# Expert products of a decoder trunk: three float32r products of halves become one plain float32 product

## Chip, cores and metric

One core of one Trainium2 chip runs the whole program. The metric is device time in microseconds (us) of that core for one launch, both layers of the trunk included; lower is better.

## What is computed

The program runs a trunk of two layers over 256 tokens of width 1024. Each layer has a mixer (four head groups) and a channel part, PEER: 8 heads choose 16 of 16384 single-neuron experts per token, and their outputs are summed. With `t` the 256 x 1024 normed activations:

```python
q = (t @ w_q).reshape(T, PEER_HEADS, 2, PEER_DKEY // 2)          # 1024 -> 2048
s1 = einsum('thd,kd->thk', q[:, :, 0], sk1)                      # 128 keys each side
s2 = einsum('thd,kd->thk', q[:, :, 1], sk2)
# top 16 of each side, top 16 of the 256 sums -> expert, gate (softmax)
a = einsum('td,thkd->thk', t, u_tab[expert])
w = gate * gelu(a)
y = einsum('thk,thkd->td', w, v_tab[expert])
```

The kernel doesn't gather. It multiplies all 16384 rows of `u_tab` with `t`, applies gelu, multiplies by a gate grid that is zero for experts not chosen, and multiplies by all of `v_tab`. All is float32. Before each layer, six modulation vectors (`silu(c) @ ada_w`, 1024 x 6144) are needed.

## The kernel before

All large weights lie in one stream of blocks of 128 x 1024 float32 (512 KB). SP fetches them in order into a ring of 4 slots (`ring`), each fetch behind a semaphore that says that the slot's block was used. Per layer there are 33 blocks for the mixer, 16 for `w_q` (query blocks), 128 for `u_tab` (expert rows) and 128 for `v_tab` (value rows). Another 48 blocks for layer 0's modulation come first; layer 1's 48 are fetched into the two slots of `ada_ring` during layer 0's value rows.

Mixer blocks are multiplied as they are, as plain float32 (lines 1278, 1290, 1478): 8 matmuls of a 128 x 128 weight with a 128 x 256 moving tile (`hT`, the normed activations, or `ynT`).

Query, expert and value blocks are multiplied in halves. A number is split in a float32r part (`hi`) and the rest (`lo`, float32r too), and each product is three float32r matmuls, hi x hi, hi x lo, lo x hi (`exact`, lines 1487 to 1491). ScalarE writes `split_hi` from the ring (`high`, line 688; line 763 for value rows). GpSimd subtracts to write `split_lo` for query and expert blocks and the first four value blocks (line 471), VectorE for the other value blocks (line 1169). The moving side is split, too: `h_hi` and `h_lo` by VectorE once a layer (1078, 1079), `w_hi` by ScalarE (757, 764) and `w_lo` by VectorE (1163, 1170) per value block. Both halves have 4 slots. A ring slot is free when its `lo` has been written.

The order of a layer on TensorE: mixer; output projection (1478); sum of squares `ss2` (1233); query blocks, each pair followed by the key scores of the pair before it (1507), which ScalarE copies out (531); expert rows in 16 turns of 8 blocks, each pair of blocks followed by a gelu on ScalarE (715) into `grid`, while VectorE chooses the top 16s from `scores`; gate grids (1556), made from one-hot tiles of VectorE (1135, 1137), ScalarE (740, 743) and GpSimd (482), which VectorE multiplies into `grid` (1142); value rows, which accumulate in four banks of PSUM that a product with `zeros` opens (1569); then VectorE adds the result to `xT` (1179). Each engine has its own instruction queue, in the order written.

In layer 0's value rows (loops of 20 blocks) GpSimd multiplies the eight `ada_ring` blocks of each of six turns by `silu(c)` and adds them to `ada_acc` (493 to 498). TensorE then sums the columns (`ada_sums`, 1241). In layer 0's own modulation at the start VectorE does it with one fused operation per block (841, 843).

`tables` (relative bias and rotary tables) and `KM` (masks) lie where the halves lie. So `tables` is spilled to DRAM in layer 0 and read back for layer 1, and `KM` is loaded twice.

Of the kernel before, what the change touches and what calls it, by code (L numbers as in the profile page):

```python
# [18 lines left out]
F32 = mybir.dt.float32  # L19
F32R = mybir.dt.float32r  # L20
# [6 lines left out]
P = 128  # L27
# [23 lines left out]
RING = 4  # L51
SPLIT = 4
# [19 lines left out]
EARLY = PQ + KEYS + SPLIT  # L72
LATE = KEYS - SPLIT
# [84 lines left out]
def build(nc, stream, s5w, consts, mixc, small, vec, pos, x_in, out):  # L158
    with ExitStack() as ctx:
# [17 lines left out]
        split_hi = at_byte("split_hi", 16 * KB, [SPLIT, BLOCK], F32R)  # L177
        split_lo = at_byte("split_lo", 32 * KB, [SPLIT, BLOCK], F32R)
        tables = at_byte("tables", 16 * KB, [HEADS * (P + T) + 3 * T])
        KM = at_byte("KM", 26 * KB, [N_MIXC])  # L180
        s5raw = at_byte("s5raw", 32 * KB, [1024])

        hT = at_byte("hT", 48 * KB, [KT, T])
        h_hi = at_byte("h_hi", 48 * KB, [KT, T], F32R)
        w_hi = at_byte("w_hi", 48 * KB, [SPLIT, T], F32R)
        w_lo = at_byte("w_lo", 52 * KB, [SPLIT, T], F32R)

        stage = at_byte("stage", 56 * KB, [2048])
        h_lo = at_byte("h_lo", 56 * KB, [KT, T], F32R)
# [130 lines left out]
        ge = at_byte("ge", 32 * KB, [FIRST, P + T], F32R)  # L320
# [58 lines left out]
        spilled, mixc_in, tables_in = (sem(n) for n in ("spilled", "mixc_in", "tables_in"))  # L379
        ada_used, ada_scaled, ada_columns = (sem(n) for n in ("ada_used", "ada_scaled", "ada_columns"))  # L380
        ada_filled = [sem(f"ada_filled{i}") for i in range(2)]
        hi_ready, lo_ready, h_split = sem("hi_ready"), sem("lo_ready"), sem("h_split")
        vhi_ready, v_ready, v_used = sem("vhi_ready"), sem("v_ready"), sem("v_used")
        hot_eq, hot_step, column_ready, turned_picks = (sem(n) for n in ("hot_eq", "hot_step", "column_ready", "turned_picks"))
        spill = nc.dram_tensor("spill", (P, HEADS * (P + T) + 3 * T), F32).ap()
# [7 lines left out]
        def early_at(l):  # L393

            return mix_at(l) + MIX


        @block.sync
        def _(sp):
# [26 lines left out]
            for l in range(DEPTH):  # L426
                segment(mix_at(l) + RING, MIX, block_used, l * MIX)
                segment(early_at(l) + RING, EARLY, lo_ready, l * EARLY)
                late = early_at(l) + EARLY
                if l + 1 == DEPTH:  # L430
                    segment(late + RING, LATE - RING, v_ready, l * KEYS + SPLIT)
                    break

                sp.wait_ge(w_ready, T // 4 * (l + 1))
                ada_turns = (0, 1, 4, 6, 8, 10, 12, 14)
                with sp.Fori(0, ADA // KT, 1) as i:
                    for j in range(20):
                        sp.wait_ge(v_ready, i * 20 + (l * KEYS + SPLIT + j + 1))
                        fetch(i * 20 + (late + RING + j), (late + RING + j) % RING)
                        if j in ada_turns:  # L440
                            k = ada_turns.index(j)
                            sp.wait_ge(ada_used, i * 8 + (ADA + k - 1))
                            sp.dma_start(ada_ring[:, k % 2, :], stream[bass.ds(i * 8 + (N_MAIN + l * ADA + k), 1)]
                                         .rearrange("o p c -> (o p) c")).then_inc(ada_filled[k % 2], 16)
                segment(late + RING + 120, LATE - 120, v_ready, l * KEYS + SPLIT + 120)
# [6 lines left out]
        def _(pool):  # L452
            gp = nc.gpsimd
            for l in range(DEPTH):
# [12 lines left out]
                e0 = early_at(l)  # L467

                def low(i, j):
                    pool.wait_ge(hi_ready, i * SPLIT + (l * EARLY + j + 1))  # L470
                    gp.tensor_tensor(split_lo[:, j, :], ring[:, (e0 + j) % RING, :], split_hi[:, j, :].bitcast(F32), ALU.subtract)\  # L471
                        .then_inc(lo_ready, 1)

                with pool.Fori(0, EARLY // SPLIT, 1) as i:
                    for j in range(SPLIT):
                        low(i, j)

# [6 lines left out]
                if l + 1 < DEPTH:  # L484

                    with pool.Fori(0, ADA // KT, 1) as i:
                        for k in range(KT):
                            pool.wait_ge(ada_filled[k % 2], i * (16 * KT // 2) + 16 * (k // 2 + 1))
                            silu = siluc[:, k:k + 1].broadcast_to([P, BLOCK])
                            if k == 0:  # L490

                                pool.wait_ge(ada_columns, i + ADA // KT)
                                gp.tensor_tensor(ada_acc[:, :], ada_ring[:, 0, :], silu, ALU.mult).then_inc(ada_used, 1)
                            else:
                                b = ada_ring[:, k % 2, :]
                                gp.tensor_tensor(b, b, silu, ALU.mult).then_inc(ada_scaled, 1)
                                pool.wait_ge(ada_scaled, i * (KT - 1) + k)
                                gp.tensor_tensor(ada_acc[:, :], ada_acc[:, :], b, ALU.add).then_inc(ada_used, 1)  # L498
                            pool.wait_ge(ada_used, i * KT + (ADA + k + 1))
# [16 lines left out]
        def _(act):  # L516
# [55 lines left out]
            for l in range(DEPTH):  # L572
                act.wait_ge(small_in, 16)
                if l:

                    act.wait_ge(v_used, l * KEYS)
                act.dma_start(s5raw[:, :], s5w[l]).then_inc(s5w_in, 16)
                if l:
                    act.dma_start(KM[:, :], mixc).then_inc(mixc_in, 16)
                    act.dma_start(tables[:, :], spill).then_inc(tables_in, 16)  # L580
# [92 lines left out]
                if l == 0:  # L673
                    act.wait_ge(t5_ready, HEADS)
                    act.wait_ge(rope_ready, 1)
                    act.dma_start(spill, tables[:, :]).then_inc(spilled, 16)

# [3 lines left out]
                e0 = early_at(l)  # L681
                if l == 0:
                    act.wait_ge(spilled, 16)

                def high(n, i=0, turn=0):

                    act.wait_ge(slot_filled[(e0 + n) % RING], i * (16 * turn // RING) + 16 * ((e0 + n) // RING + 1))
                    nc.scalar.activation(split_hi[:, n % SPLIT, :], ring[:, (e0 + n) % RING, :], ACT.Copy).then_inc(hi_ready, 1)  # L688


                for n in range(SPLIT - 1):
                    high(n)
                root(l, "ss2", D, rstd)
                for k in range(KT):
                    act.wait_ge(xr_ready, 2 * KT * l + KT + k + 1)
                    nc.scalar.activation(sq[:, k, :], sq[:, k, :], ACT.Identity, bias=mod2[:, l, 3 * KT + k:3 * KT + k + 1],
                                         scale=sc2[:, k:k + 1]).then_inc(h_ready, 1)
                high(SPLIT - 1)
                for h in range(PH + 1):
                    for w in range(2):  # L700
                        if h < PH:
                            copy(l, f"pq{h}_{w}", qT[:, 2 * (h % 2) + w, :])
                            high(2 * h + w + SPLIT)
# [6 lines left out]
                def gelus(i):  # L710
                    for j in range(4):
                        act.wait_ge(a_ready, i * 4 + (first + j + 1))
                        for w in range(2):
                            high(PQ + 2 * j + w + SPLIT, i, 8)
# [39 lines left out]
                act.wait_ge(w_ready, T // 4 * (l + 1))  # L754
                late = e0 + EARLY
                for j in range(SPLIT):
                    nc.scalar.activation(w_hi[:, j, :], grid[:, j * T:j * T + T], ACT.Copy).then_inc(vhi_ready, 1)
                with act.Fori(0, LATE // SPLIT, 1) as i:
                    for j in range(SPLIT):
                        s = (late + j) % RING  # L760
# [967 lines left out]
```

## Time and profile before

| | us |
|---|---|
| median of 3 runs | 2529.12 (2522.28 to 2531.38) |
| span of the profiled execution | 2525.9 |
| TensorE busy (matmul records) | 2230.9, 88% |
| VectorE busy | 1553.5, 62% |
| ScalarE busy | 1185.2, 47% |
| GpSimd busy | 1123.5, 44% |
| bytes moved | 378.58 MB, mean 150 GB/s |

The profiled execution's span lies 3.2 us below the median of the runs. Stages in its time: modulation and tables to 130, mixer and output projection to 337, query blocks 347 to 414, expert rows to 784, gate grids to 910, value rows to 1344; then the same without the first: mixer to 1569, query blocks 1579 to 1646, expert rows to 2016, gate grids to 2142, value rows to 2511, final norm to 2526. Of the profile's page, the chain of waits gives 19% to GpSimd's `split_lo` and 7% to each of the three product lines. In the rows below the engines are PE (TensorE's matmuls), PEld (its weight loads), DVE (VectorE), ACT (ScalarE), POOL (GpSimd) and SP (SyncE, which issues the DMAs).

### The profile page before, as it was taken

Reading aid. Unit: us, or ns where it says so; the run is one execution under the profiler, and the core shown is the slowest. Engines: PE = TensorE matmul, PEld = TensorE weight load, DVE = VectorE, ACT = ScalarE, POOL = GpSimd, SP = SyncE. Lnnn points to the kernel's source line nnn. Section 1 sums busy time; section 2 is a strip of 40 time slices with the busy share of each in tenths; the row PEclk is TensorE's granted clock in tenths of the full one; section 3 lists DMA queues with packets and bytes.
Section 4 is the critical chain, followed back from the end, with each engine's and each line's share of the span. In section 5 each row is a group of like instructions: output and inputs, shape, how many; then the busy total and the mean of one; then the engine's idle time right before and its main releaser. Section 6 shows DMA issues by size and latency. Waiting matters only on the chain.

```text
span 2525.9 us, 46629 instructions
## 1 busy us (share of the span) xinstructions
PE 2230.9 (88%) x16556; PEld 2138.3 (85%) x16556; DVE 1553.5 (62%) x2319; ACT 1185.2 (47%) x2092; POOL 1123.5 (44%) x472
## 2 busy tenths in 40 slices
PE   5797789999997589999998967999999956999998
PEld 4686679999996588989997856899999955999998
DVE  7577348993004977888885952699800088555554
ACT  8522434555545743333433232455554476444443
POOL 0002036988886545555550301588988854000000
PEclk9798789999998999999998987999999999999999
DMA  7632144555553036556553312345555500555553
GB/s 264 216 115 78 45 141 134 183 179 187 183 181 102 0 116 218 206 209 224 208 215 120 125 34 92 125 151 190 181 180 181 182 17 0 175 182 182 183 183 108
DMA packets 103456, 378.58 MB, mean 150 GB/s; under 512 B 11489, under 2 KB 11873, under 8 KB 102881
## 3 DMA queue, kind: packets, MB, share of 16 engines
q1 hardware_dynamic: 102672, 373.74, 43.3%
q10 hardware_dynamic: 720, 4.00, 0.4%
q8 instruction: 40, 0.66, 0.1%
q14 instruction: 24, 0.19, 0.0%
HBM read 375.46 MB, written 2.23 MB: 150 GB/s over the span
## 4 chain that ended last, share of the span: by engine, by line
PE 34%; issue 24%; POOL 23%; DVE 12%; DMA 3%; ACT 2%; POOLq 1%; DVEq 1%; SPq 0%; ACTq 0%
POOL split_lo L471 19%; PE bank L1489 7%; PE bank L1490 7%; PE bank L1491 7%; PE bank L1556 3%; PE bank L1278 3%; POOL hots L482 2%; DVE w_lo L1170 2%; DMA ring<-stream 1%; DVE hots L1137 1%; PE bank L1241 1%; DVE split_lo L1169 1%; POOL ada_acc L498 1%; DMA ada_ring<-stream 1%; DVE hots L1135 1%
## 5 line engine op out<-in xcount | busy, mean ns | idle before, releaser
L471 POOL TENSOR_TENSOR split_lo<-ring,split_hi 128x1024 fp32r<-128x1024 f32 x296 | 729.3, 2489 | 246.6 <-ACT split_hi L688 246.3
L1489 PE MATMUL bank<-h_hi,split_hi 128*128 128x256 f32 x2304 | 657.0, 285 | 29.7 <-DVE h_lo L1079 21.3
L1490 PE MATMUL bank<-h_lo,split_hi 128*128 128x256 f32 x2304 | 654.4, 284 | 0.0
L1491 PE MATMUL bank<-h_hi,split_lo 128*128 128x256 f32 x2304 | 654.4, 284 | 0.0
L1489 PE MATMUL bank<-w_hi,split_hi 128*128 128x256 f32 x2048 | 589.4, 288 | 14.2 <-DVE w_lo L1170 14.2
L1490 PE MATMUL bank<-w_lo,split_hi 128*128 128x256 f32 x2048 | 586.8, 287 | 0.0
L1491 PE MATMUL bank<-w_hi,split_lo 128*128 128x256 f32 x2048 | 586.5, 286 | 0.0
L1169 DVE TENSOR_TENSOR split_lo<-ring,split_hi 128x1024 fp32r<-128x1024 f32 x248 | 375.3, 1513 | 251.6 <-ACT w_hi L764 251.6
L1489 PEld LDWEIGHTS bank<-h_hi,split_hi 128*128 128x128 f32 x2304 | 444.5, 193 | 34.7 <-issue 18.6
L763 ACT ACTIVATE split_hi<-ring 128x1024 fp32r<-128x1024 f32 x248 | 262.5, 1059 | 448.9 <-PE bank L1491 416.0
L1491 PEld LDWEIGHTS bank<-h_hi,split_lo 128*128 128x128 f32 x2304 | 444.8, 193 | 0.0
L1490 PEld LDWEIGHTS bank<-h_lo,split_hi 128*128 128x128 f32 x2304 | 444.8, 193 | 0.0
L688 ACT ACTIVATE split_hi<-ring 128x1024 fp32r<-128x1024 f32 x296 | 298.4, 1050 | 274.0 <-PE bank L1491 273.7
L1489 PEld LDWEIGHTS bank<-w_hi,split_hi 128*128 128x128 f32 x2048 | 400.8, 196 | 17.1 <-DVE w_lo L1170 17.1
L1490 PEld LDWEIGHTS bank<-w_lo,split_hi 128*128 128x128 f32 x2048 | 400.8, 196 | 0.1
L1491 PEld LDWEIGHTS bank<-w_hi,split_lo 128*128 128x128 f32 x2048 | 400.6, 196 | 0.0
L1135 DVE TENSOR_TENSOR hots<-K,pick 128x256 f32<-128x256 f32 x64 | 54.1, 846 | 307.4 <-ACT pick L732 224.5
L1556 PE MATMUL bank<-hots 128*128 128x128 f32 x1024 | 137.8, 291 | 105.8 <-POOL hots L482 105.8
L1556 PEld LDWEIGHTS bank<-hots 128*128 128x128 f32 x1024 | 126.5, 202 | 117.1 <-DVE grid L1142 88.3
L1170 DVE TENSOR_TENSOR w_lo<-grid,w_hi 128x256 fp32r<-128x256 f32 x248 | 188.6, 760 | 0.0
L482 POOL TENSOR_TENSOR hots<-hots,pick 128x1024 f32<-128x1024 f32 x64 | 123.3, 1928 | 103.9 <-DVE hots L1137 103.9
L740 ACT ACTIVATE hots<-K,pick 128x128 f32<-128x128 f32 x384 | 119.1, 388 | 56.0 <-PE bank L1556 56.0
(267 smaller groups left out, 2776.9 us busy)
## 6 DMA issues: line engine op xcount, KB each, us to landing
ring<-stream SPq DMA_DIRECT2D x658, 512.0 KB, 3.3
ada_ring<-stream SPq DMA_DIRECT2D x48, 512.0 KB, 4.8
spill<-tables ACTq DMA_DIRECT2D x1, 1152.0 KB, 5.4
tables<-spill ACTq DMA_DIRECT2D x1, 1152.0 KB, 7.2
xT<-x_in SPq DMA_DIRECT2D x1, 1024.0 KB, 10.2
s5raw<-s5w ACTq DMA_DIRECT2D x2, 512.0 KB, 5.7
y_out<-hT SPq DMA_DIRECT2D x1, 1024.0 KB, 3.9
KM<-mixc SPq DMA_DIRECT2D x1, 576.0 KB, 8.3
```

The source lines that it names most:

```text
L471: gp.tensor_tensor(split_lo[:, j, :], ring[:, (e0 + j) % RING, :], split_hi[:, j, :].bitcast(F32), ALU.subtract)\
L482: gp.tensor_tensor(hotA[j], hotA[j], pick[:, 2, bass.ds(i * 16 + 8 * j, 8)].unsqueeze(2).broadcast_to([P, 8, P]), ALU.mult).then_inc(hot_r ...
L688: nc.scalar.activation(split_hi[:, n % SPLIT, :], ring[:, (e0 + n) % RING, :], ACT.Copy).then_inc(hi_ready, 1)
L740: last = nc.scalar.activation(hotB[j][:, t, :], iota, ACT.Abs, scale=-1.0, bias=pick[:, 1, bass.ds(n * 8 + t, 1)])
L763: nc.scalar.activation(split_hi[:, j, :], ring[:, s, :], ACT.Copy)
L1135: v.tensor_tensor(hotB[j][:, 0:2, :], iota.unsqueeze(1).broadcast_to([P, 2, P]), pick[:, 1, bass.ds(n * 8, 2)].unsqueeze(2).broadcast_to([ ...
L1169: v.tensor_tensor(split_lo[:, j, :], ring[:, (late + j) % RING, :], split_hi[:, j, :].bitcast(F32), ALU.subtract)
L1170: v.tensor_tensor(w_lo[:, j, :], grid[:, bass.ds(i * (SPLIT * T) + (SPLIT + j) * T, T)], w_hi[:, j, :].bitcast(F32), ALU.subtract).then_in ...
L1489: mm(dst, hi, x_hi, start=start, stop=False, skip_group_check=not group)
L1490: mm(dst, hi, x_lo, start=False, stop=False, skip_group_check=not group)
L1491: return mm(dst, lo, x_hi, start=False, stop=stop, skip_group_check=not group)
L1556: last = mm(bank[:, j, t * P:t * P + P], hotB[j // 2][:, s, :], hotA[j // 2][:, s, :], start=True, stop=True)
```

## The change

The three products of halves become one plain float32 matmul of the ring's block with `hT` (query and expert rows) or with `grid` (value rows). The second sub-layer's norm is written to `hT` instead of `sq`. All splits go, on ScalarE, GpSimd and VectorE. The space of `split_hi` goes to the ring, which has 8 slots; the ring's fetches now all wait for `block_used`, which TensorE raises. `tables` and `KM` get a place of their own for the whole run: no spill, no reload. `s5raw` moves to the bytes of `hots0`, `ge` to those of `stage` and its neighbours. Layer 1's modulation moves from GpSimd to VectorE, with one fused operation per block; turns of value rows have 16 blocks instead of 20, and each `ada_ring` load is issued behind every second fetch.

```diff
-RING = 4
-SPLIT = 4
+RING = 8
+TURN = 16
@@ SP @@
-                    for j in range(20):
-                        sp.wait_ge(v_ready, i * 20 + (l * KEYS + SPLIT + j + 1))
-                        fetch(i * 20 + (late + RING + j), (late + RING + j) % RING)
-                        if j in ada_turns:
-                            k = ada_turns.index(j)
+                    for j in range(TURN):
+                        sp.wait_ge(block_used, i * TURN + (freed + MIX + PQ + KEYS + j + 1))
+                        fetch(i * TURN + (v0 + RING + j), (v0 + RING + j) % RING)
+                        if j % 2 == 0:
+                            k = j // 2
                             sp.wait_ge(ada_used, i * 8 + (ADA + k - 1))
                             sp.dma_start(ada_ring[:, k % 2, :], stream[bass.ds(i * 8 + (N_MAIN + l * ADA + k), 1)]
@@ ScalarE @@
-                    act.wait_ge(v_used, l * KEYS)
+                    act.wait_ge(w_ready, T // 4 * l)
                 act.dma_start(s5raw[:, :], s5w[l]).then_inc(s5w_in, 16)
-                if l:
-                    act.dma_start(KM[:, :], mixc).then_inc(mixc_in, 16)
-                    act.dma_start(tables[:, :], spill).then_inc(tables_in, 16)
...
-                    nc.scalar.activation(sq[:, k, :], sq[:, k, :], ACT.Identity, bias=mod2[:, l, 3 * KT + k:3 * KT + k + 1],
+                    nc.scalar.activation(hT[:, k, :], sq[:, k, :], ACT.Identity, bias=mod2[:, l, 3 * KT + k:3 * KT + k + 1],
@@ VectorE, value rows @@
-                            v.tensor_tensor(split_lo[:, j, :], ring[:, (late + j) % RING, :], split_hi[:, j, :].bitcast(F32), ALU.subtract)
...
+                if l + 1 < DEPTH:
+                    with dve.Fori(0, ADA // KT, 1) as i:
+                        for k in range(KT):
+                            dve.wait_ge(ada_filled[k % 2], i * (16 * KT // 2) + 16 * (k // 2 + 1))
...
+                                ins = v.scalar_tensor_tensor(ada_acc[:, :], ada_ring[:, k % 2, :], siluc[:, k:k + 1], ada_acc[:, :],
+                                                             ALU.mult, ALU.add)
@@ TensorE @@
-                        last = exact(dst, hi[:, k, :], lo[:, k, :], h_hi[:, k, :], h_lo[:, k, :], k == 0, k == KT - 1)
+                        last = mm(dst, b[:, k, :], hT[:, k, :], start=(k == 0), stop=(k == KT - 1))
...
-                            last = exact(bank[:, 4 + m // 2, (m % 2) * T:(m % 2) * T + T], split_hi[:, s, c], split_lo[:, s, c],
-                                         w_hi[:, s, :], w_lo[:, s, :], False, False, group=False)
-                        last.then_inc(v_used, 1)
+                            last = mm(bank[:, 4 + m // 2, (m % 2) * T:(m % 2) * T + T], ring[:, slot, m * P:m * P + P],
+                                      grid[:, bass.ds(i * (n * T) + j * T, T)], start=False, stop=False, skip_group_check=True)
+                        last.then_inc(block_used, 1)
```

## Rows read from the trace of the kernel before

**Rows 1.** The page: GB/s moved, in 40 equal slices of the span.
```profile
GB/s 264 216 115 78 45 141 134 183 179 187 183 181 102 0 116 218 206 209 224 208 215 120 125 34 92 125 151 190 181 180 181 182 17 0 175 182 182 183 183 108
```

**Rows 2.** Busy time by stretch: length, busy us (records) per engine, clock, DMA share, GB/s.
```profile
415.00:788.00 373.00, 368.98 (x3075) 368.71 (x3073) 176.93 (x305) 195.59 (x227) 315.05 (x128) 1.00 0.54 179
910.00:1344.00 434.00, 403.91 (x3167) 399.86 (x3167) 344.19 (x249) 169.30 (x248) 224.97 (x90) 0.95 0.59 208
2142.00:2512.00 370.00, 368.99 (x3074) 368.76 (x3072) 194.70 (x251) 169.65 (x250) 0.00 (x0) 1.00 0.50 170
```

**Rows 3.** TensorE in order of time, expert rows: start, length, what, [idle before].
```profile
414.34 0.39 PE L1489 MATMUL bank<-h_hi,split_hi 128*128 128x256 f32 x1 [0.47 <-ACT grid L531]
...
700.02 0.28 PE L1489 MATMUL bank<-h_hi,split_hi 128*128 128x256 f32 x1
700.14 0.28 PE L1490 MATMUL bank<-h_lo,split_hi 128*128 128x256 f32 x1
```

**Rows 4.** Lines 1278 and 1478 alone: records, ns min/median/max, first and last start.
```profile
L1278 PE MATMUL bank<-hT,ring x512: 379/379/796, 130.0 to 1448.8; 128*128 128x256 f32 x171
...
L1478 PE MATMUL bank<-hT,ring x256: 379/379/796, 304.0 to 1566.2; 128*128 128x256 f32 x128
```

**Rows 5.** TensorE in order of time, mixer of layer 0.
```profile
153.46 13.98 PE L1278 MATMUL bank<-hT,ring 128*128 128x256 f32 x64
167.28 3.62 PE L1303 MATMUL bank<-grid,ring 128*128 128x256 f32 x16
170.73 7.31 PE L1290 MATMUL bank<-ring,hT 128*128 128x128 f32 x64
```

**Rows 6.** TensorE's groups, 910 to 1344 us: records, busy, mean ns, idle before.
```profile
L1489 PE MATMUL bank<-w_hi,split_hi 128*128 128x256 f32 x1024 | 299.4, 292 | 14.2 <-DVE w_lo L1170 14.2
...
L1241 PE MATMUL bank<-K,ada_acc 128*128 128x1 f32 x96 | 15.8, 294 | 15.9 <-POOL ada_acc L498 15.9
```

**Rows 7.** Busy time by stretch behind two of the six column sums, columns as before.
```profile
978.00:980.00 2.00, 2.00 (x12) 2.00 (x11) 0.00 (x0) 0.00 (x0) 0.00 (x0) 0.50 0.85 283
...
1047.00:1050.00 3.00, 3.00 (x16) 3.00 (x16) 1.14 (x2) 0.00 (x0) 0.00 (x0) 0.50 0.91 285
```

**Rows 8.** Order of time at three handoffs: mixer, query blocks, gate grids of layer 0.
```profile
130.01 1.22 PE L1278 MATMUL bank<-hT,ring 128*128 128x256 f32 x2 [6.96 <-ACT hT L588]
...
346.94 0.55 PE L1489 MATMUL bank<-h_hi,split_hi 128*128 128x256 f32 x1 [8.94 <-DVE h_lo L1079]
...
784.01 2.00 ACT L688 ACTIVATE split_hi<-ring 128x1024 fp32r<-128x1024 f32 x2 [3.27 <-PE bank L1491]
...
785.92 0.58 ACT L715 ACTIVATE grid<-bank 128x512 f32 x1
786.40 1.85 ACT L740 ACTIVATE hots<-K,pick 128x128 f32<-128x128 f32 x6
...
788.28 0.84 ACT L743 ACTIVATE hots<-hots 128x768 f32<-128x768 f32 x1
...
789.95 4.73 POOL L482 TENSOR_TENSOR hots<-hots,pick 128x1024 f32<-128x1024 f32 x2
792.92 6.01 PE L1556 MATMUL bank<-hots 128*128 128x128 f32 x32 [8.95 <-POOL hots L482]
```

**Rows 9.** Line 1137 alone, ns min/median/max.
```profile
L1137 DVE TENSOR_TENSOR hots<-K,pick x64: 1209/1212/3422, 741.7 to 2132.4; 128x1024 f32<-128x1024 f32 x64
```

**Rows 10.** Line 843 alone, and its idle time before (us, times).
```profile
L843 DVE SCALAR_TENSOR_TENSOR grid<-ring,tiny,grid x42: 1278/1285/1286, 22.5 to 99.0; 128x1024 f32 x42
...
  DMA ring<-stream: 6.4, 12
```

**Rows 11.** DMA issues: count, KB each, median us to landing.
```profile
ring<-stream SPq DMA_DIRECT2D x658, 512.0 KB, 3.3
ada_ring<-stream SPq DMA_DIRECT2D x48, 512.0 KB, 4.8
```

**Rows 12.** Line 1241 alone: the register operations of TensorE's sequencer.
```profile
L1241 PEldq FUSED_REGOPS  x48: 42/46/51, 974.3 to 1317.0; - x48
```

## What the change should do

> **What bounds the kernel now.** I read four views, in this order. The first is the table by stretch [rows 2], which tells what each stage costs and which engine fills it. In the expert products of layer 0 (415 to 788 us) TensorE is busy 369 of 373 us at granted clock 1.00, and in the value products of layer 1 (2142 to 2512) 369 of 370 us. GpSimd is busy 315 of 373 us in the first and not at all in the second, and the time per block is the same. So GpSimd, which the chain of waits names most often, is close behind but is not the limit: TensorE is. A block there is 24 matmuls. The value products of layer 0 take 434 us for the same 128 blocks, because they also hold the next layer's modulation sums.
>
> Second is the order of instructions on TensorE. In a dense stretch a float32r matmul starts every 0.12 us [rows 3], so a block costs 24 x 0.12 = 2.88 us. Check against the stage: 128 blocks x 2.88 = 368.6 us, and layer 1's value products keep TensorE busy for 369.0 us [rows 2].
>
> Third is the price of what replaces them, a plain float32 128x128 by 128x256 matmul. The mixer's projections are just that, from the same ring and with the same moving tile hT. Here the count must be read before the duration. Line 1278 is called for 16 projections per layer, 8 matmuls each, 2 layers: 256 matmuls. The trace has 512 records [rows 4]. Line 1478 has 8 x 8 x 2 = 128 matmuls and 256 records [rows 4]. So one plain float32 matmul is two records, each with its own weight load. 64 records start from 153.46 and the next line's from 167.28 [rows 5]: 13.82 / 64 = 0.216 us for a record, 0.432 us for a matmul, 8 x 0.432 = 3.455 us for a block. The trap is to read 0.216 us as a whole matmul.
>
> Beside the rows: the Trainium skill, "FP8 and Floating Point Precision", section "TensorE Precision Notes", says that true FP32 takes 4 passes through the array. By that rule alone a block would be 32 passes against the 24 of the three-product form, a third more. The rows give 3.455 / 2.88 = 1.20, since the float32r matmul with its 0.120 us is dearer than a quarter of 0.432. Sum by the rule's ratio: 544 blocks x 0.96 us = +522 us instead of +313. The measured pace decides, and I go by it.
>
> **The change part by part.**
>
> (a) Products. Each of the 544 blocks (per layer 16 query blocks, 128 expert rows, 128 value rows) goes from 2.88 to 3.455 us of TensorE, +0.575. Where TensorE is the limit this is all on the path. Expert rows: layer 0 runs from 414.34 to 783.97 (the first grid matmul at 792.92 less its 8.95 idle) [rows 3, 8], 369.6 us; new 128 x 3.455 = 442.3. +73 a layer, +146 for both. Value rows of layer 1: 369 to 442.3, +73.5.
>
> (b) Halves. On ScalarE, GpSimd and VectorE 544 `split_hi`, 296 + 248 `split_lo` and 248 pairs of `w_hi`/`w_lo` go away. The busiest of the three, GpSimd, took 315.05 / 128 = 2.46 us per block [rows 2] beside TensorE's 2.88, so removing them returns only the 14.2 us that TensorE waited for `w_lo` in layer 0's value rows [rows 6]. What is late next is TensorE itself.
>
> (c) Value rows of layer 0. Now 434 us [rows 2]: 368.6 of products, 15.8 of column sums (line 1241), 15.9 waiting for `ada_acc`, 14.2 for `w_lo` [rows 6]; the remaining 19.5 us is what the clock costs after the pauses. It stands near 0.50 for 3 to 7 us behind them (two such stretches: [rows 7]), where a product takes twice as long. After the change the sums move from GpSimd to VectorE, one fused operation per block. The same form takes 1.28 us [rows 10], so 8 are 10 us in a turn of 55 us: hidden. The wait doesn't go, however. The eighth `ada_ring` load is issued only when block 14 of the turn is used, and only block 15 (3.46 us) stands before the sums. SP's two issues and its wake are about 0.5 us, an estimate, the landing 4.8 us [rows 11], the operation 1.28, some 0.2 for semaphores, an estimate too: 6.8 us, so a stall of 3.3 us, x 6 = 20 us. Bounds: 2 us each if it lands in the ring's 3.3 [rows 11], so 12, and 4.5 each, so 27. I keep the clock's 19.5 us, since pause and column sums stay as long. New: 442.3 + 15.8 + 20 + 19.5 = 497.6, +63.6 (55 to 75). SP queues the ring's next fetch ahead of the late load and nothing urgent behind it, with eight slots ahead.
>
> (d) Query stage. Now 67.4 us (346.94 to 414.34). New: 16 x 3.455 = 55.3; the keys' 64 records a layer at 0.114 us, the pace of 64 plain 128-column records in the mixer [rows 5], 7.3; half clock at the start about 2, waits for ScalarE's copies about 4, both estimates: 68.6. +1 a layer, between -4 and +4.
>
> (e) Handoff to the query stage. Now TensorE idles 8.94 us behind `h_lo`, while the same chain without halves at the start of the mixer costs 6.96 us [rows 8]. -2 a layer, -4; the later waits for `h_lo` (about 1.8 us a layer) are inside the range.
>
> (f) Start of the gate grids. The last products end at 783.97, yet ScalarE's last gelu starts at 785.92, since two `split_hi` stand before it; the first grid waits for GpSimd's `hots`, behind two `split_lo`, at 789.95 [rows 8]. Without these: gelu 0.58, six one-hots 1.85 and the Relu 0.84, about 3.4 us to the first grid matmul. VectorE's one-hot line 1137 took up to 3.42 us, just there, against 1.21 normally [rows 9], and its GpSimd neighbour is gone, too. -5.5 a layer, -11 (-4 to -12). By the Trainium skill, "SBUF — State Buffer", section on the two separate sides, a GpSimd operation and certain VectorE ones hold a shared port exclusively; the 3.42 us fits, and elsewhere in the change it touches nothing on the path. The rest of the grid stage (one turn of 7 us per two quads) has the same operations.
>
> (g) Ring of 8, at the start: VectorE's fused operations wait 6.4 us for the ring [rows 10], and the plain ones before them 2 to 3 more. Eight slots may take half of it, while `pos` now shares its landing with more loads: -4 (-9 to +3). A block of 0.524 MB per 3.455 us is 152 GB/s, less than the 170 to 208 of the stages now [rows 2], so no stage becomes bound by transfers; with 48 more in (c) it is 185.
>
> (h) The spill, its reload, KM's reload and their waits: no wait for them is among TensorE's or VectorE's in these stretches, so 0 (-2 to 0).
>
> (i) The moving operand of the value rows is now addressed by a register. No row shows that on TensorE; the nearest is line 1241 on `ada_acc`, one register operation of 46 ns per matmul [rows 12]. Its upper bound is 2048 x 0.046 = 94 us. Line 1241's 96 records still take only 15.8 us [rows 6], 0.33 us a matmul with clock losses, and 46 ns fits into 432: 0.
>
> Sum: 146 + 73.5 + 63.6 + 2 - 4 - 11 - 4 = +266. Profiled span 2525.9 + 266 = 2792 us; the median of runs lies 3.2 us above the profiled span, so **2795 us**.
>
> **Rivals.**
> A, not slower: one float32 matmul is one record of 0.216 us, so a block costs 1.73 us. Transfers would bound it before that: 0.524 MB at 264 GB/s, the fastest slice of the profile [rows 1], is 1.99 us. 544 x (2.88 - 1.99) = 484 us less, some 2045 us. It decides at a block cost of 2.88 us, that is 0.36 us a matmul. For it: GpSimd, the chain's top entry, is freed. Against: 512 records for 256 calls, and the same for line 1478. 2%.
> B: register addressing of the moving operand isn't hidden, up to +94, so up to 2889. Against: line 1241's pace. 4%.
> C: layer 0's value rows go without stall and clock loss, since the turn is regular and GpSimd no longer feeds them: -39, 2756. Against: the load that is issued one block ahead. 6%.
> D: a price that follows the count of passes (4 to 3) as in the four products of halves against three: +0.96 us a block instead of 0.575, 544 x 0.385 = +209, some 3000 us. Against: the measured pace of line 1278 under traffic. 2%.
>
> **How the numbers follow.** Forecast as summed 86%. The bounds together: (c) -8 to +11, (d) +-8, (f) -1 to +7, (g) -5 to +7, expert rows +-6. Added as independent about +-18, and widened for what I can't see; with C the range reaches 2755 to 2835. A measurement of this kernel can tell about 0.5% from no change; 2795 is 10.5% above. Slower 0.97, within 0.5% 0.01, faster 0.02.
>
> **What would show it.** In the profile of the changed kernel: 16 records per block at 0.216 us on the two product lines (4096 records for the value rows and 4608 for query and expert rows); expert rows about 442 us with TensorE busy throughout at clock 1.00; 6 stalls of about 3.3 us at the column sums with the clock at 0.5 behind each; GpSimd with no work in expert and value rows; first grid matmul 3.4 us after the last product. 8 records per block would prove A; gaps of 40 to 50 ns between value matmuls B.

## The result

The changed kernel takes 2779.6 us (median of 4 runs, 2774.2 to 2784.7) against 2525.7 us for the kernel before (4 runs). The ratio is 1.101, with a 95% interval of 1.098 to 1.103. The forecast of 2795 us was 0.6% too high, and the time lies in the forecast range of 2755 to 2835 us. The profiled execution has a span of 2779.5 us, 253.6 more than before. The page of the changed kernel, parts 1 to 4, first lines (line 1412 is the query and expert product, line 1500 the value product, 1475 the gate grids, 1160 the column sums):

```profile
span 2779.5 us, 33968 instructions
...
PE 2527.7 (91%) x12204; PEld 2210.0 (80%) x12204; DVE 882.6 (32%) x1831; ACT 533.8 (19%) x1268; POOL 167.3 (6%) x86
...
PE 81%; DVE 9%; issue 3%; ACT 2%; POOL 2%; DMA 1%; DVEq 0%; SPq 0%; POOLq 0%; ACTq 0%
PE bank L1412 36%; PE bank L1500 32%; PE bank L1475 2%; PE bank L1197 2%; PE bank L1397 2%; POOL hots L465 2%; DVE hots L1057 1%; PE bank L1160 1%; DVE grid L774 1%; DMA ada_ring<-stream 1%; PE bank L1371 1%; PE bank L1152 1%; DVE hots L1055 1%; PE bank L1422 1%; PE bank L1222 0%
```

Every engine except TensorE has lost much of its work: ScalarE 1185 to 534 us, GpSimd 1124 to 167, VectorE 1554 to 883. TensorE has 297 us more, and now it holds 81% of the chain. So a quarter fewer matmul records (16556 to 12204) cost more time, since a plain record takes 0.216 us and a float32r record 0.120.

The table by stretch of the changed kernel (length, busy us and records of PE, PEld, DVE, ACT, POOL, then granted clock, DMA share, GB/s), for layer 0's expert rows, layer 0's value rows and layer 1's value rows, which answer to [rows 2]:

```profile
404.00:847.00 443.00, 442.90 (x2054) 389.60 (x2054) 93.22 (x307) 55.57 (x80) 1.90 (x1) 1.00 0.46 152
966.00:1463.00 497.00, 479.47 (x2146) 419.46 (x2144) 58.90 (x50) 0.00 (x0) 0.00 (x0) 0.95 0.54 185
2322.00:2764.00 442.00, 442.00 (x2050) 389.09 (x2049) 0.00 (x0) 0.00 (x0) 0.00 (x0) 1.00 0.44 143
```

TensorE in order of time, layer 1's value rows, which answers to [rows 3, 5]:

```profile
2322.31 442.19 PE L1500 MATMUL bank<-grid,ring 128*128 x2048
```

The two product lines alone (records, ns min/median/max, first and last start), which answer to [rows 4]:

```profile
L1500 PE MATMUL bank<-grid,ring x4096: 379/379/774, 966.2 to 2764.1; 128*128 x196
...
L1412 PE MATMUL bank<-hT,ring x4608: 379/379/795, 335.7 to 2202.3; 128*128 128x256 f32 x192
```

There are 16 records per block, 4096 for 256 value blocks and 4608 for 288 query and expert blocks, and 442.19 / 2048 = 0.216 us per record. Neither line waits inside a stage: the 4608 records of line 1412 have 14.9 us of idle time before them in total, almost all of it at the two starts.

Where the 253.6 us come from, stage by stage, worked out from the first starts and the idle times in both traces:

| stage | before | after | difference | forecast |
|---|---|---|---|---|
| start to output projection, layer 0 | 304.0 | 294.6 | -9.4 | -4 |
| output projection to query blocks, layer 0 | 43.0 | 41.1 | -1.9 | -2 |
| query blocks, both layers | 134.8 | 135.8 | +1.0 | +2 |
| expert rows, layer 0 / 1 | 369.6 / 369.6 | 443.0 / 443.0 | +73.3 / +73.3 | +73 / +73 |
| gate grids, layer 0 / 1 | 125.9 / 126.0 | 119.3 / 119.6 | -6.6 / -6.4 | -5.5 / -5.5 |
| value rows, layer 0 | 434.6 | 496.5 | +61.9 | +63.6 |
| mixer to query blocks, layer 1 | 234.6 | 229.5 | -5.1 | -2 |
| value rows, layer 1 | 369.0 | 442.2 | +73.2 | +73.5 |

### The profile page after: what moved, and what is told of

Read it like the earlier page. It is cut to its first block, busy times and chain, and to the rows that moved or that the text cites. A ratio compares the mean times of both kernels' runs of the same rounds, so it can differ in the third digit from the quotient of the medians.

```text
span 2779.5 us, 33968 instructions
## 1 busy us (share of the span) xinstructions
PE 2527.7 (91%) x12204; PEld 2210.0 (80%) x12204; DVE 882.6 (32%) x1831; ACT 533.8 (19%) x1268; POOL 167.3 (6%) x86
## 3 DMA queue, kind: packets, MB, share of 16 engines
q10 hardware_dynamic: 288, 1.05, 0.1%
HBM read 373.70 MB, written 1.05 MB: 135 GB/s over the span
## 4 chain that ended last, share of the span: by engine, by line
PE 81%; DVE 9%; issue 3%; ACT 2%; POOL 2%; DMA 1%; DVEq 0%; SPq 0%; POOLq 0%; ACTq 0%
PE bank L1412 36%; PE bank L1500 32%; PE bank L1475 2%; PE bank L1197 2%; PE bank L1397 2%; POOL hots L465 2%; DVE hots L1057 1%; PE bank L1160 1%; DVE grid L774 1%; DMA ada_ring<-stream 1%; PE bank L1371 1%; PE bank L1152 1%; DVE hots L1055 1%; PE bank L1422 1%; PE bank L1222 0%
## 5 line engine op out<-in xcount | busy, mean ns | idle before, releaser
L1412 PE MATMUL bank<-hT,ring 128*128 128x256 f32 x4608 | 1002.7, 380 | 14.9 <-ACT hT L643 13.9
L1412 PEld LDWEIGHTS bank<-hT,ring 128*128 128x128 f32 x4608 | 877.5, 191 | 135.5 <-ACT hT L643 14.7
L1500 PE MATMUL bank<-grid,ring 128*128 x4096 | 902.0, 384 | 0.0
L1500 PEld LDWEIGHTS bank<-grid,ring 128*128 128x128 f32 x4096 | 789.5, 193 | 110.2
L658 ACT ACTIVATE grid<-bank 128x512 f32 x128 | 76.4, 597 | 625.6 <-PE bank L1412 625.3
L1197 PE MATMUL bank<-hT,ring 128*128 128x256 f32 x512 | 119.5, 396 | 16.0 <-ACT hT L552 13.9
L1089 DVE SCALAR_TENSOR_TENSOR ada_acc<-ada_ring,tiny,ada_acc 128x1024 f32<-128x1024 f32 x42 | 54.0, 1285 | 236.6 <-DMA ada_ring<-stream 236.6
L1197 PEld LDWEIGHTS bank<-hT,ring 128*128 128x128 f32 x512 | 101.4, 199 | 33.9 <-ACT hT L552 14.7
L1062 DVE TENSOR_TENSOR grid<-grid,bank 128x512 f32 (+1 forms) x128 | 87.9, 688 | 25.4 <-PE bank L1475 24.6
L1171 PE MATMUL bank<-ge,diag 128*128 128x384 f32 x248 | 54.0, 366 | 36.9 <-ACT diag L522 25.4
L1171 PEld LDWEIGHTS bank<-ge,diag 128*128 128x128 f32 x248 | 45.8, 203 | 44.8 <-issue 25.8
L1057 DVE TENSOR_TENSOR hots<-K,pick 128x1024 f32<-128x1024 f32 x64 | 77.6, 1213 | 0.0
L1397 PE MATMUL bank<-hT,ring 128*128 128x256 f32 x256 | 60.1, 400 | 1.4 <-ACT hT L477 1.4
## 6 DMA issues: line engine op xcount, KB each, us to landing
KM<-mixc SPq DMA_DIRECT2D x1, 576.0 KB, 11.1
```

The lines of the kernel that those rows point to most:

```text
L658: nc.scalar.activation(grid[:, bass.ds(i * (8 * T) + j * 2 * T, 2 * T)], bank[:, j, :], ACT.Gelu_apprx_tanh).then_inc(gelu_done, 1)
L1057: v.tensor_tensor(hotA[j], iota.unsqueeze(1).broadcast_to([P, 8, P]), pick[:, 0, bass.ds(n * 8, 8)].unsqueeze(2).broadcast_to([P, 8, P]), ...
L1062: v.tensor_tensor(gw, gw, bank[:, b, :].rearrange("p (t a) -> p a t", t=4), ALU.mult).then_inc(w_ready, 1)
L1171: last = mm(bank[:, 2 + q, 0:P + T], diag[:, j, q, part, :], ge[:, slot, :], start=isinstance(b, int) and b + part == 0, stop=False, skip_ ...
L1197: last = mm(r, b[:, k, :], hT[:, k, :], start=(k == 0), stop=(k == KT - 1))
L1397: last = mm(r, b[:, k, :], ynT[:, k, :], start=(k == 0), stop=(k == KT - 1))
```

## Experiments

Each ran against the kernel before on the same chip. Theory: TensorE's price per block sets the stages with products; pauses at the column sums come from the late load and cost their own length and a stretch of half clock; the deeper ring helps at the start only. The rivals are those of the prediction and, for the kernel before, that GpSimd was the limit.

### One part alone: plain products in layer 1's value rows of the kernel before

```diff
...
+                            for m in range(KT):
+                                last = mm(bank[:, 4 + m // 2, (m % 2) * T:(m % 2) * T + T], ring[:, s, m * P:m * P + P],
+                                          grid[:, bass.ds(i * (SPLIT * T) + (SPLIT + j) * T, T)], start=False, stop=False,
+                                          skip_group_check=True)
+                            last.then_inc(v_used, 1)
```

(and the loops that make the halves of these blocks taken out; TensorE waits for the ring's slot itself, and SP's fetches wait for `v_used`)

> The kernel before with one part of the change: layer 1's value blocks 4 to 127 as plain float32 matmuls from the ring (4 slots), without their halves; all else as before. Theory (only TensorE's price per block counts): 124 x 0.575 = +71 us, the value rows from 369 to 440, 2526 + 71 = 2597 in all. Rival (the halves on ScalarE and VectorE had cost something in hidden waits or contention, so that the net is smaller): under +60.

Measured: 2596.6 us against 2525.4, ratio 1.027 (1.025 to 1.030), so +71 us. The new line alone, in that kernel:

```profile
L1600 PE MATMUL bank<-grid,ring x1984: 377/379/381, 2153.4 to 2581.4; 128*128 x199
L1600 PEldq FUSED_REGOPS  x124: 46/46/65, 2151.5 to 2574.3; - x124
```

1984 records for 124 blocks, from 2153.4 to the end of the last at about 2581.7: 3.454 us a block. The price shows by itself, with the ring of 4 and everything else of the kernel before. The halves of these blocks are gone from ScalarE and VectorE, and no gain from that comes off it: the rival (under +60 us) falls.

### The moving operand at a fixed address

```diff
-                                      grid[:, bass.ds(i * (n * T) + j * T, T)], start=False, stop=False, skip_group_check=True)
+                                      grid[:, j * T:j * T + T], start=False, stop=False, skip_group_check=True)
```

> The changed kernel with the moving operand of the value rows at an address that doesn't depend on the loop's register (it reads the same 16 columns of the grid in every turn, so the sum is another). Theory (the register operation is hidden under the 0.432 us of a matmul): 442 us for layer 1's value rows, 2780 in all. Rival B of the prediction (it costs up to 46 ns a matmul): 2048 x 0.046 = 94 us less, 2686.

Measured: 2773.5 us (two runs) against the changed kernel's 2779.6. Layer 1's value rows in order of time, in this kernel:

```profile
2315.43 442.19 PE L1500 MATMUL bank<-grid,ring 128*128 128x256 f32 x2048
```

The same 442.19 us as with the register. The 6 us between the two kernels are the width of the spread of the runs (2774 to 2785), and in the profiled executions they lie in layer 0's value rows (490.6 instead of 496.5 us), where the clock falls at other moments. Rival B falls. The records of the sequencer also show that its premise was wrong: 124 register operations for 124 blocks above, and 256 for 256 blocks in the changed kernel, one per block and not one per matmul.

### A ring of 4 slots in the changed kernel

```diff
-RING = 8
+RING = 4
...
-                    pe.wait_ge(slot_filled[slot], i * 16 + 16 * (n // RING + 1))
+                    pe.wait_ge(slot_filled[slot], i * (16 * 8 // RING) + 16 * (n // RING + 1))
...
-                    for j in range(RING):
+                    for j in range(8):
```

> The changed kernel with a ring of 4 slots again. Theory (the deeper ring helps only at the start, where VectorE waited 9.1 us for blocks): the query stage starts 8 to 10 us later, 2788 to 2790 in all, expert and value rows unchanged at 443, 496 and 442 us. Rival (the ring isn't what shortened the start; the order of the first loads is): within 2 us of 2780. Rival (with 4 slots the 3.46 us blocks also stall in layer 0's value rows, where two streams share the transfers): 10 to 30 us there.

Measured: 2782.2 us median (2779.3 to 2794.1, 5 runs), ratio to before 1.101 (1.099 to 1.104). In the profiled execution the query stage starts at 345.35 us instead of 335.72, and VectorE waits for the ring again. Waits of VectorE, 15 to 110 us, with 4 slots:

```profile
DVE grid L774 <- DMA ring<-stream: 7.9, 15, 1.0
...
DVE grid L772 <- DMA ring<-stream: 1.4, 2, 0.7
```

With 8 slots that view has no wait for the ring in this stretch. So the 9.4 us at the start are the ring's by the profiles. The medians don't show it: they differ by 2.6 us only, which their spreads don't tell apart, and the expected 2788 to 2790 us was missed. The profile with 4 slots is also that of its slowest run. Layer 0's value rows take 498 instead of 497 us, with 19.2 instead of 17.2 us at the column sums: the second rival falls, too.

### The modulation loads earlier, in the changed kernel

```diff
-                        if j % 2 == 0:
-                            k = j // 2
+                        if j in (0, 1, 2, 4, 6, 8, 10, 12):
+                            k = (0, 1, 2, 4, 6, 8, 10, 12).index(j)
```

> The changed kernel with the eight loads of layer 1's modulation blocks issued behind fetches 0, 1, 2, 4, 6, 8, 10, 12 of a turn instead of 0, 2, ..., 14. Value rows of layer 0 take 496.5 us in the changed kernel: 442.2 of products, 20.3 of column sums, 17.2 of waiting for ada_acc, 16.8 left over, which I put down to the clock. Theory (the late load is what TensorE waits for, and its pause is what lowers the clock): the wait goes to 0, the leftover goes too, and the sums take 12: 455 to 462, the run at about 2742. Rival 1 (the sums with one moving column lower the clock by themselves): only the wait goes, 479, the run at about 2762. Rival 2 (VectorE's own sums are late, not the load): nothing moves, 2780.

Measured: 2737.4 us (4 runs), ratio to before 1.084 (1.081 to 1.086), 42 us less than the changed kernel. First the changed kernel around a column sum, in order of time and by stretch (0.50 is 1.2 GHz, 1.00 is 2.4 GHz):

```profile
1016.12 1.28 DVE L1089 SCALAR_TENSOR_TENSOR ada_acc<-ada_ring,tiny,ada_acc 128x1024 f32<-128x1024 f32 x1 [5.53 <-DMA ada_ring<-stream]
1018.90 0.33 SPq L436 DMA_DIRECT2D ada_ring<-stream  x1
...
1023.07 1.28 DVE L1089 SCALAR_TENSOR_TENSOR ada_acc<-ada_ring,tiny,ada_acc 128x1024 f32<-128x1024 f32 x1 [5.67 <-DMA ada_ring<-stream]
1024.49 3.57 PE L1160 MATMUL bank<-K,ada_acc 128*128 128x1 f32 x16 [2.90 <-DVE ada_acc L1089]
```

```profile
1021.00:1024.00 3.00, 0.59 (x3) 0.19 (x1) 0.93 (x1) 0.00 (x0) 0.00 (x0) 0.99 0.84 292
1024.00:1028.00 4.00, 3.51 (x17) 3.51 (x17) 0.36 (x1) 0.00 (x0) 0.00 (x0) 0.50 0.11 43
1028.00:1031.00 3.00, 3.00 (x9) 2.44 (x9) 0.00 (x0) 0.00 (x0) 0.00 (x0) 0.53 0.00 0
```

The last load is issued at 1018.90, VectorE can start on it 4.2 us later, and TensorE's pause until it has finished is 2.90 us. Then the clock stands at its lower level for some 7 us: the sum takes 3.57 us, and 9 product records fall in 3 us, where the run with earlier loads has 16 in a stretch of the same length. Behind the first two of the six pauses the lower level lasts about 7 us, behind the other four about 10. The third sum starts at 1151.13, and the clock has fallen before that, while TensorE still does nothing (busy 0.00):

```profile
1150.00:1151.00 1.00, 0.00 (x0) 0.00 (x0) 0.99 (x1) 0.00 (x0) 0.00 (x0) 0.63 0.95 369
```

So it is in five of the six turns; in the second the clock falls during the sum. With the earlier loads, the same views (two of the six sums, and the stretches around the first):

```profile
1020.72 1.84 PE L1160 MATMUL bank<-K,ada_acc 128*128 128x1 f32 x16
1077.76 1.84 PE L1160 MATMUL bank<-K,ada_acc 128*128 128x1 f32 x16
```

```profile
1020.00:1023.00 3.00, 3.00 (x24) 2.85 (x23) 0.00 (x0) 0.00 (x0) 0.00 (x0) 1.00 0.43 122
1023.00:1026.00 3.00, 3.00 (x16) 2.64 (x15) 0.00 (x0) 0.00 (x0) 0.00 (x0) 1.00 0.24 97
```

No pause, full clock through the sum, and the six sums follow each other at 57.04 us: 55.34 for 16 blocks and 1.70 from the first matmul of a sum to the next product. Value rows take 453 us (1.00, busy throughout) instead of 496.5. So rival 1 falls: the one-column sums don't lower the clock by themselves. The pause of 2.8 to 3.0 us goes ahead of the fall each time, and it costs more than its own length: 17.2 us of waiting stood for 43.5, of which 9 lay in the sums (20.3 to 11.1) and 17 in the products behind them. Not every such pause lowers it at once: behind the value rows the changed kernel pauses 3.39 us before the sum of squares, and the clock stays at 1.00 through it.

### The same shift in the kernel before

```diff
-                ada_turns = (0, 1, 4, 6, 8, 10, 12, 14)
+                ada_turns = (0, 1, 3, 5, 7, 9, 11, 12)
```

> The kernel before with the eight loads of layer 1's modulation blocks behind fetches 0, 1, 3, 5, 7, 9, 11, 12 of the 20 of a turn instead of 0, 1, 4, 6, 8, 10, 12, 14. There TensorE waits 15.9 us for ada_acc in layer 0's value rows and some 19.5 us more go to the clock behind it. Theory (the late load is the cause here, too, and the clock follows the pause): the last load comes two blocks, 5.8 us, earlier against waits of 2.65 us each, so up to 35 us less, 2490. Rival (GpSimd's own 5.3 us per block is what is late, in a turn where it waits 16 us for its first load but not for its last): the wait stays or shrinks by a third, 2515 to 2525. Rival (the fetch queue blocks on the ada slot and the ring of 4 runs dry): slower than 2530.

Measured: 2503.5 us (2495.6 to 2510.9, 6 runs) against 2525.8, ratio 0.992 (0.990 to 0.995). The wait for `ada_acc` is gone, as the theory says, and value rows take 410.5 us instead of 434.6. But the expected 35 us came to 22 in the run and 24 in this stage. TensorE's waits in that stretch:

```profile
PE bank L1489 <- DVE w_lo L1170: 21.4, 19, 2.2
```

It was 14.2 us [rows 6], so 7 us of the gain went into a wait that was there before. And of the 20 us that were left over in this stage, 9 stay. The granted clock still falls three times, for 3.4 us each and each time around a wait for `w_lo` of 2.0 to 2.2 us. That is some 5 us of lost products, an estimate; the other 4 have no account. ScalarE's waits for the ring grew from 32.9 to 80.2 us; the ring of 4 with its fetches behind the crowded loads is a likely reason for the longer waits, but no run tests it. This version is 0.8% faster than the kernel before, with the same three products, and beats the changed one.

### Two products instead of three, in the kernel before

```diff
                     mm(dst, hi, x_hi, start=start, stop=False, skip_group_check=not group)
-                    mm(dst, hi, x_lo, start=False, stop=False, skip_group_check=not group)
                     return mm(dst, lo, x_hi, start=False, stop=stop, skip_group_check=not group)
```

> The kernel before without the second of the three products (high half of the block by low half of the moving side), in query, expert and value rows; all halves are still made. It leaves that part of the sum out. TensorE's block falls from 2.88 to 16 x 0.12 = 1.92 us. Theory (TensorE was the limit, and GpSimd with 2.46 us is next in expert rows, VectorE with 1.51 + 0.76 = 2.27 in value rows): expert rows 128 x 2.6 = 333 instead of 370, value rows of layer 1 about 300 instead of 369; 2526 - 74 - 69 - 10 to 30 = about 2360. Rival (GpSimd was already the limit, as the chain's 19% suggests): expert rows stay at 370. Rival (halves cost nothing at all): 246 us for each stage, 2526 - 0.96 x 544 = 2004.

Measured: 2245.4 us, ratio 0.890 (0.885 to 0.896). By stretch: layer 0's query and expert rows, and layer 1's value rows.

```profile
342.00:715.00 373.00, 327.90 (x2374) 300.82 (x2374) 275.38 (x479) 223.79 (x273) 350.00 (x143) 0.97 0.60 199
1995.00:2234.00 239.00, 239.00 (x1994) 238.99 (x1992) 190.72 (x245) 165.90 (x244) 0.00 (x0) 1.00 0.81 263
```

144 query and expert blocks take 371 us instead of 437, with GpSimd busy 94% of it. The 128 expert rows alone take 318.5 instead of 369.6 us: 2.49 us a block, GpSimd's own pace (2.46 before). So GpSimd was second, 0.4 us a block behind TensorE, and it is the limit once TensorE's share falls. It was not the limit before, or this stage would not have moved. In layer 1's value rows, where VectorE makes the low halves, TensorE is busy throughout and 1994 records fill 239 us, 0.120 us each: 1.92 us a block, so there TensorE is still the limit. My 2.27 us for VectorE was too high there: its 190.72 us for the 245 operations of this stretch are 1.56 us a block. That stage gives 123 us where the forecast of this run had 69, and query and expert rows give 131 where it had 74. Together they are 111 of the 115 us between 2360 and 2245.

Layer 0's value rows gave only 19 us (415.7 instead of 434.6). TensorE waits 74.5 us there for VectorE's `w_lo`. VectorE is slower in that stage, where GpSimd works beside it. In the kernel before, its subtraction alone, in layer 0's value rows and then in layer 1's (count, busy us, mean ns, idle before):

```profile
L1169 DVE TENSOR_TENSOR split_lo<-ring,split_hi 128x1024 fp32r<-128x1024 f32 x124 | 223.2, 1800 | 83.4 <-ACT w_hi L764 83.4
...
L1169 DVE TENSOR_TENSOR split_lo<-ring,split_hi 128x1024 fp32r<-128x1024 f32 x124 | 152.1, 1227 | 168.2 <-ACT w_hi L764 168.2
```

So in layer 0's value rows VectorE was the close second before, with 2.78 us a block (344.19 / 124 [rows 2]) against 2.88.

### One product of the high halves

```diff
-                    mm(dst, hi, x_hi, start=start, stop=False, skip_group_check=not group)
-                    mm(dst, hi, x_lo, start=False, stop=False, skip_group_check=not group)
-                    return mm(dst, lo, x_hi, start=False, stop=stop, skip_group_check=not group)
+                    return mm(dst, hi, x_hi, start=start, stop=stop, skip_group_check=not group)
```

(and the loops that make the low halves of blocks and of `w` taken out; the waits that named a low half, SP's fetches among them, name the high half)

> The kernel before with only the product of the two high halves, and no low halves of blocks made (GpSimd's and VectorE's subtractions are gone, w_lo too). It leaves the other two products out. TensorE 8 x 0.12 = 0.96 us per block, ScalarE 1.05 for the half and 0.3 to 0.37 for the gelu or w_hi. Theory (transfers bound it next): at the 264 to 315 GB/s of the fastest slices a block takes 1.66 to 1.99 us, so expert rows 213 to 255 us, value rows the same, about 1950 to 2050 in all. Rival (the handover between ScalarE and ring with 4 slots bounds it, since a transfer takes 3.3 us to land): 128 x 3.5 / 4 + waits, under 200 us. Rival (ScalarE's chain): 128 x 1.4 = 180 us.

Measured: 1860.3 us, ratio 0.737 (0.735 to 0.740). By stretch: layer 0's query and expert rows, its value rows, layer 1's value rows.

```profile
342.00:597.00 255.00, 183.81 (x1222) 162.53 (x1221) 133.70 (x475) 215.99 (x267) 1.90 (x1) 0.93 0.82 286
722.00:1030.00 308.00, 189.01 (x1114) 177.56 (x1113) 0.21 (x1) 162.90 (x248) 190.30 (x90) 0.73 0.80 289
1640.00:1845.00 205.00, 159.06 (x1032) 136.94 (x1031) 0.00 (x0) 163.99 (x248) 0.00 (x0) 0.96 0.87 307
```

The expected 1950 to 2050 us was missed. No compute engine is full: TensorE has 184 of 255 us, ScalarE 216. The DMA share is 0.80 to 0.87, and 286 to 307 GB/s arrive in all three, with 332 in the fastest slice of its page. A block takes 1.60 to 1.77 us (layer 0's value rows count 176, with the modulation's), below the 1.99 of rival A's bound, which took the 264 GB/s of one slice [rows 1] for a limit. So TensorE is no longer the limit, and transfers are the likely one, but that isn't shown. In layer 0's query and expert rows ScalarE waits only 21.2 us for the ring, so it is close to the limit itself. And a ring load lands in 4.9 us here instead of 3.3: with 4 slots and 1.05 us of ScalarE for each, the handover rival gives (4.9 + 1.05) / 4 = 1.5 us a block, an estimate near the measured pace. No run with a deeper ring tells the two apart. This version computes with the rounding of float32r in all three kinds of block; where that is enough, it is the fastest by far.

## Why the prediction held, point by point

**What bounds the kernel.** TensorE was the limit in the product stages. Adding 0.575 us a block to TensorE, with less work for all others, moved them by 0.573 (73.3 / 128), and taking 0.96 away moved the expert rows by 0.40, down to GpSimd's pace. The chain's 19% for `split_lo` was a close second's share.

**(a), the price of a block.** Two records per plain matmul is the step that carried the forecast: with 0.216 us read as a whole matmul, rival A came to 484 us less, not 254 more. The 3.455 us came out in three kernels (the changed one, the one with the fixed address, the one with plain products in layer 1's value rows alone). Rival A and rival D (passes counted without durations) both fall. "FP8 and Floating Point Precision" of the Trainium skill, section "TensorE Precision Notes", by its 4 passes, has the direction right; the ratio is 1.20 here and not 4 / 3, as each float32r matmul takes 0.120 us where half a plain record takes 0.108.

**(b), halves.** Right in the main: the engines' 650 to 960 us of busy time came back as little more than the 14 us of waits. Two readings were off. The busiest of the three isn't GpSimd everywhere: in layer 0's value rows it is VectorE, 2.78 us a block, since its subtraction takes 1.80 us there and 1.23 in layer 1, without GpSimd beside it. So (f)'s remark that this neighbour touches nothing on the path elsewhere doesn't hold: the 14.2 us of waits for `w_lo` are all in that stage, and layer 1's value rows have none. And four of the ten stretches at the lower clock in that stage begin just behind a wait for `w_lo` of 1.9 to 2.0 us (one is 1022 to 1026 us, granted clock 0.60), so the halves had a share in the 19.5 us that (c) put down to pause and sums.

**(c), layer 0's value rows.** 497.6 forecast, 496.5 measured. Inside, the stall was 17.2 instead of 20, mainly because the load lands in 4.2 us instead of 4.8. The sums took 20.3 instead of 15.8, since five of the six now run at half clock throughout (3.57 us; in the kernel before they took 1.94 to 3.47). The leftover was 16.8 instead of 19.5. The errors cancel, so that the sum came out within 1.1 us is luck. Rival C named what was to be had, but the earlier load was needed for it.

**(d), (e).** +1.0 and -1.9 against +2 and -2. The wait between norm and first product is 6.95 us, the one of the mixer [rows 8].

**(f), gate grids.** The pause before the first grid is 3.49 us in the profile, as forecast. ScalarE's Relu, not GpSimd, ends it now. The changed kernel in order of time:

```profile
847.03 0.60 ACT L658 ACTIVATE grid<-bank 128x512 f32 x1 [6.31 <-PE bank L1412]
...
849.40 0.84 ACT L686 ACTIVATE hots<-hots 128x768 f32<-128x768 f32 x1
...
850.39 5.20 PE L1475 MATMUL bank<-hots 128*128 128x128 f32 x32 [3.49 <-ACT hots L686]
```

VectorE's one-hot line alone:

```profile
L1057 DVE TENSOR_TENSOR hots<-K,pick x64: 1209/1212/1221, 793.6 to 2312.5; 128x1024 f32<-128x1024 f32 x64
```

VectorE's one-hot takes 1.22 us at most now, against 3.42 at worst beside GpSimd [rows 9]: "SBUF — State Buffer" of the Trainium skill, section "SBUF: two separate sides", on the port that these two share, agrees. The stage gained 6.6 and 6.4 us, 1 us more than (f) gave; which of the next grids brought it wasn't followed up.

**(g), the start.** The term that was mis-sized most: -9.4 instead of -4, just outside its own bounds of -9 to +3. The whole wait for the ring went, not half of it, and `pos` landed no later (VectorE waits 4.6 us for it instead of 5.0). The run with 4 slots shows that it is the ring.

**What was not forecast.** 3 us between the value rows of layer 0 and the mixer of layer 1: in the kernel before the sum of squares there took 6.7 us at half clock, and 3.7 us in the changed one. In the changed kernel with earlier loads the same takes 5.4 us, so it depends on when the clock falls around the preceding pause of 3.39 us, and nothing shows it as a property of the change.

Total: the forecast's +266 against +253.6; 5.4 us of the difference is (g), 3.1 layer 1's mixer with the clock behind layer 0, 2.0 the gate grids, 1.7 (c) (0.6 of it because the stage before took 434.6 and not 434), 1.0 the query blocks, less some 0.5 for stages slightly over their forecast. Another 3 us of the 15 between 2795 and 2779.6 are the 3.2 that the forecast added for the distance of median and profiled span, which was a chance of few runs: it is 0.1 in the changed kernel.

## What to carry to other kernels

Count the records of an operation against its calls before its duration is used: here one plain float32 matmul is two records, and float32 costs 1.20 times three float32r products. When one engine is the limit by a small margin, as TensorE's 2.88 against GpSimd's 2.46 us here, freeing the others gives next to nothing, and only a cut of the first shows what the second allows. Ask for the second by stage: here it was GpSimd in expert rows and VectorE in layer 0's value rows. A short pause of TensorE in a dense stage is worth removing beyond its own length, since here the lower clock behind it took as much again and more (43.5 us for 17.2); issue the load that feeds it by its landing time, not by an even spacing.

## What the runs showed of the hardware

- A float32r matmul with 256 moving columns starts every 0.120 us in dense stages, a plain float32 one every 0.432 us in two records of 0.216, at granted clock 1.00. A float32r matmul is 11% dearer than half of a plain record (0.108 us), and three of them (0.360 us) are still cheaper than one plain matmul.
- Pauses of 2.8 to 3.0 us ahead of one-column sums went with a fall of the granted clock from 1.00 to 0.50 in all six turns of the changed kernel, for some 7 us twice and some 10 us four times; in five turns it fell before the sum began. The same sums without a pause left it at 1.00 in all six turns. In the kernel before, as it is and with earlier loads, waits of 1.9 to 2.2 us in the products were followed by 3.4 us at 0.50 several times.
- VectorE's subtraction of two 128 x 1024 tiles takes 1.23 us without GpSimd at work and 1.80 us on average beside it (kernel before, value rows of layers 1 and 0).
- Register addressing of the moving operand costs TensorE nothing here (442.19 us with and without), and takes one 46 ns operation of its sequencer per block of 8 matmuls.
- One core's transfers reached 307 GB/s over 205 us and 332 in one slice (the version with one product), where no slice of the kernel before shows more than 264.
